# Decode values of a hybrid decoder layer: two samples share one 128-row operand, one value sum per pair, loads issued by ScalarE

## The chip, the cores and the metric

One core of a Trainium2 chip runs the kernel. The metric is device time in microseconds (us) of one execution, lower is better. Engine names: PE (TensorE, matmuls), DVE (VectorE), ACT (ScalarE), POOL (GpSimd), SP (SyncE, which here only issues DMAs).

## What is computed

One inference step of a decoder layer, for a prompt of 256 tokens and for 8 samples with one new token each (264 token columns in all, `T`): a half-step SwiGLU FFN, a combined projection `h @ w_in`, dilated attention in three head groups of four heads, a complex-diagonal SSM, gates, an output projection and a second half-step FFN. The part that is changed is the decode attention of the samples, more exactly its product with the cached values:

```
idx = buf_len + arange(S)[:, None] - arange(n_back + 1)[None, :] * dil
kg, vg = k_all[:, idxc], v_all[:, idxc]
s = einsum('bshe,bsjhe->bhsj', q, kg) * ATT_SCALE
p, lse = masked_softmax_lse(s, valid)
o = einsum('bhsj,bsjhe->bshe', p, vg)
```

For each of the 8 samples and each of the three groups (dilation 1, 4, 16) 128 cached keys and the new one count; the three groups' outputs of a head slot are merged by their softmax denominators. The kernel normalizes over the three groups at once, so the merged output of one sample and one head is a single sum over 3 x 128 cached keys of weight times value (128 wide), plus the new token's term.

## The kernel before

**The slab stream.** All weights pass as slabs of 512 x 256 f32 (512 KB). `put` (L399) on SP issues a slab's load into one of four buffers `raw`; ACT rounds it to `w_hi` (`split_hi`, L611); DVE makes the rest, `w_lo = raw - w_hi` (`split_lo`, L1002); PE does three matmuls for each of 8 tiles (24 in all, `slab_products`, L1440 to L1442). ACT and DVE work on the slab three places ahead of PE (`LEAD`). ACT's split of place j waits until PE is done with the slab before place j, so ACT's body for place j begins about when PE begins slab j.

**The phase `gates_b`.** Four iterations i of eight slabs j (0 to 7). Into them, at fixed places written out by hand in each engine's body, two other pieces of work are threaded, each for k = 2i (half h = 0) and k = 2i + 1 (h = 1).

The SSM piece of block k: PE multiplies the inputs after slab j = 1 or 4 (L1741, `su_done`); ACT copies the product out and prepares states (L843 to L847, `sv_ready`); POOL (L2056 to L2060) and DVE (L1264 to L1267) make the real and the imaginary part of the scan input; DVE runs two scans (L1271, L1273, `scan_ready`), the second after POOL's `zr_ready`; then POOL (L2062, L2064, L2068, `xr_ready`) and DVE (L1282, L1283, L1289, `xi_ready`) turn the scan output into `xs`, with DVE's `w_lo` of a slab (L1002) ahead of its share; PE waits for both and makes the outputs after slab j = 4 or 7 (`y_products`, L1713 and L1719).

The value piece of sample k: SP loads three tiles `vu`, 128 keys x 512 each (L550, 256 KB), at j = 1 and 5; ACT scales the 12 head columns by their weights in `pt_dec` (L828) at j = 0 and 3; POOL adds the three groups in two steps (L2049, L2051) at the head of each half, before its SSM part; PE sums over the 128 keys with four products against a column of ones (L1752) after slab j = 2 and j = 5; DVE adds the new token's term (`add_values`, L1251). There are two sets of three tiles.

The order on each engine is the order of its body: POOL does half 0, then half 1; a wait in it holds all that is behind it. The first phase after `gates_b`, `attn_branch`, waits for `att_lo` (L1299), made on DVE from the samples' attention output.

## Time and profile before

| | |
|---|---|
| median of 3 runs | 2247.19 us (2247.15 to 2248.25) |
| the profiled execution's own time | 2247.63 us |
| its span, first to last instruction | 2244.6 us |
| granted TensorE clock | 1.00 |
| PE / DVE / ACT / POOL busy | 2234.5 / 1373.5 / 995.5 / 488.1 us |
| `gates_b` to the first product of the next phase | 1172.65 to 1294.35 us |

The profile gives, for one execution, the busy time of each engine, the chain of work that ended last, and groups of instructions with their duration and with what ended the idle time before them. Its time lines give start and duration (us) of each instruction. A duration in a time line is from issue to end, so an instruction that stands blocked after its issue shows as a longer one. Matmuls overlap: their spacing counts, not their duration.

### The profile page before, as it was taken

What the parts mean: (1) busy time and instruction counts of PE and PEld (TensorE: products, weight loads), DVE (VectorE), ACT (ScalarE), POOL (GpSimd) and SP (SyncE); (2) the same over time, 40 slices, a digit from 0 to 9 for tenths busy, and PEclk for the clock granted to TensorE, in tenths of its full rate; (3) what the DMA queues carried; (4) which work ended last, traced back from release to release, by engine and by line L of the source; (5) the groups of instructions that cost most, each with busy time, mean ns of one, the idle gap of its engine ahead of it and who ended that gap; (6) DMA issues with size and microseconds to landing.
All of it is one profiled execution on the core that took longest, in us unless ns stands there. A gap on an engine that the chain in (4) does not pass through costs nothing.

```text
span 2244.6 us, 48634 instructions
## 1 busy us (share of the span) xinstructions
PE 2234.5 (100%) x19149; PEld 2223.3 (99%) x19149; DVE 1373.5 (61%) x1434; ACT 995.5 (44%) x1247; POOL 488.1 (22%) x530
## 2 busy tenths in 40 slices
PE   9999999999999999999999999999999999999999
PEld 8999999999999999999999999999999999999999
DVE  7556456665455757876659867665554555545555
ACT  6554334334344544444455665444343343433443
POOL 2587013320000206764306630100000000000000
PEclk9999999999999999999999999999999999999999
DMA  7878678887786688769858875578877788777764
GB/s 226 264 243 259 193 235 271 262 249 239 234 249 202 220 264 262 219 188 298 291 185 285 266 231 182 174 232 251 247 237 226 240 246 256 229 228 242 242 201 147
DMA packets 441036, 528.53 MB, mean 235 GB/s; under 512 B 41360, under 2 KB 421696, under 8 KB 437088
## 3 DMA queue, kind: packets, MB, share of 16 engines
q1 hardware_dynamic: 425600, 508.57, 72.4%
q0 software_dynamic: 3248, 11.62, 1.5%
q10 hardware_dynamic: 12080, 6.83, 1.0%
q8 instruction: 76, 1.25, 0.2%
q14 instruction: 32, 0.26, 0.0%
HBM read 507.80 MB, written 106.09 MB: 273 GB/s over the span
## 4 chain that ended last, share of the span: by engine, by line
PE 97%; DVE 2%; issue 0%; ACT 0%; DMA 0%; ACTq 0%; DVEq 0%
PE pa L1440 31%; PE pa L1441 31%; PE pa L1442 31%; DVE w_lo L1002 1%; PE pb L1618 0%; PE pb L1713 0%; DVE xg_lo L1019 0%; PE pb L1719 0%; PE pb L1678 0%; PE pb L1656 0%; PE pb L1636 0%; PE pb L1752 0%; DMA vec_rows<-in_ffn_norm 0%; DVE x_t L1026 0%; PE pb L1741 0%
## 5 line engine op out<-in xcount | busy, mean ns | idle before, releaser
L1002 DVE TENSOR_TENSOR w_lo<-raw,w_hi 128x1024 fp32r<-128x1024 f32 x735 | 934.7, 1282 | 624.0 <-ACT w_hi L611 620.0
L1440 PE MATMUL pa<-xg_hi,w_hi 128*128 128x264 f32 x3968 | 1135.4, 286 | 1.9 <-DVE w_lo L1002 1.7
L1441 PE MATMUL pa<-xg_lo,w_hi 128*128 128x264 f32 x3968 | 1127.8, 284 | 0.0
L1442 PE MATMUL pa<-xg_hi,w_lo 128*128 128x264 f32 x3968 | 1126.3, 284 | 0.0
L611 ACT ACTIVATE w_hi<-raw 128x1024 fp32r<-128x1024 f32 x735 | 768.8, 1056 | 760.0 <-PE pa L1442 713.9
L1440 PEld LDWEIGHTS pa<-xg_hi,w_hi 128*128 128x128 f32 x3968 | 747.0, 188 | 5.2 <-DVE w_lo L1002 2.5
L1441 PEld LDWEIGHTS pa<-xg_lo,w_hi 128*128 128x128 f32 x3968 | 745.4, 188 | 0.6
L1442 PEld LDWEIGHTS pa<-xg_hi,w_lo 128*128 128x128 f32 x3968 | 745.9, 188 | 0.0
L1441 PE MATMUL pa<-act_lo,w_hi 128*128 128x264 f32 x1632 | 463.9, 284 | 0.0
L1440 PE MATMUL pa<-act_hi,w_hi 128*128 128x264 f32 x1632 | 463.5, 284 | 0.0
L1442 PE MATMUL pa<-act_hi,w_lo 128*128 128x264 f32 x1632 | 463.2, 284 | 0.0
L1440 PEld LDWEIGHTS pa<-act_hi,w_hi 128*128 128x128 f32 x1632 | 307.3, 188 | 0.1
L1442 PEld LDWEIGHTS pa<-act_hi,w_lo 128*128 128x128 f32 x1632 | 306.7, 188 | 0.0
L1441 PEld LDWEIGHTS pa<-act_lo,w_hi 128*128 128x128 f32 x1632 | 306.4, 188 | 0.0
L1848 POOL TENSOR_TENSOR ssq<-ssq,sq_v 128x528 f32<-128x528 f32 x12 | 19.0, 1587 | 367.7 <-ACT sq_v L622 352.3
L735 ACT ACTIVATE act_hi<-hid_v 128x528 f32 (+2 forms) x44 | 28.0, 636 | 158.3 <-DVE hid_v L1165 158.3
L1997 POOL TENSOR_TENSOR silu_v<-up_v,cs 64x264 f32<-64x264 f32 x48 | 66.9, 1394 | 93.0 <-DVE up_v L1198 89.4
L719 ACT ACTIVATE silu_v<-gate_v 128x528 f32<-128x528 f32 (+1 forms) x44 | 28.0, 637 | 108.1 <-DVE gate_v L1157 108.1
L1167 DVE TENSOR_TENSOR act_lo<-hid_v,act_hi 128x528 f32 (+2 forms) x44 | 32.2, 732 | 38.8 <-ACT act_hi L735 38.8
L1058 DVE SCALAR_TENSOR_TENSOR x_t<-pa,x_t 128x528 f32 (+1 forms) x55 | 38.9, 707 | 27.9 <-PE pa L1442 27.8
L2019 POOL TENSOR_TENSOR prod<-ku,qb 128x512 f32<-128x512 f32 x24 | 40.8, 1698 | 46.7 <-DMA qb<-q_dram 31.1
L1047 DVE TENSOR_TENSOR up_v<-pa,rstd 128x528 f32<-128x528 f32 (+1 forms) x44 | 30.5, 693 | 29.7 <-PE pa L1442 29.7
(339 smaller groups left out, 1501.0 us busy)
## 6 DMA issues: line engine op xcount, KB each, us to landing
raw<-in_ffn_w_gate SPq DMA_DIRECT2D x172, 512.0 KB, 4.8
raw<-in_ffn_w_up SPq DMA_DIRECT2D x172, 512.0 KB, 5.0
out_kv_s<-in_cache_kv_w SPq DMA_DIRECT2D x165, 512.0 KB
raw<-in_ffn_w_down SPq DMA_DIRECT2D x160, 512.0 KB, 4.5
raw<-in_w_in SPq DMA_DIRECT2D x152, 512.0 KB, 4.8
raw<-in_w_out SPq DMA_DIRECT2D x32, 512.0 KB, 4.5
tab<-ssm_tab SPq DMA_DIRECT2D x8, 1152.0 KB, 9.1
raw<-in_w_ssm_branch SPq DMA_DIRECT2D x16, 512.0 KB, 4.3
```

What stands on the lines that cost most here:

```text
L611: act.activation(w_hi[:, slot], raw[:, slot], ACT.Copy).then_inc(hi_ready, 1)
L719: act.activation(silu_v[:, 0:w], gate_v[:, 0:w], ACT.Silu).then_inc(silu_ready, 1)
L735: act.activation(act_hi[:, bass.ds(tile0, w), :], hid_v[:, 0:w], ACT.Copy).then_inc(acthi_ready, 1)
L1002: dve.tensor_tensor(w_lo[:, slot], raw[:, slot], w_hi[:, slot].bitcast(f32), ALU.subtract).then_inc(lo_ready, 1)
L1047: return dve.tensor_tensor(out, pa[:, b:b + w, 0:T], rstd[:, None, :].to_broadcast([P, w, T]), ALU.mult)
L1058: dve.scalar_tensor_tensor(x_t[:, bass.ds(2 * c, 2), :], pa[:, b:b + 2, 0:T], scale, x_t[:, bass.ds(2 * c, 2), :], ALU.mult, ALU.add).then ...
L1167: dve.tensor_tensor(act_lo[:, bass.ds(tile0, w), :], hid_v[:, 0:w], act_hi[:, bass.ds(tile0, w), :].bitcast(f32), ALU.subtract).then_inc(a ...
L1440: pe.matmul(out, wh, hi, start=first, stop=False)
L1441: pe.matmul(out, wh, lo, start=False, stop=False)
L1442: return pe.matmul(out, wl, hi, start=False, stop=last)
L1997: pool.tensor_tensor(silu_v[to:to + 64, u], up_v[frm:frm + 64, u], cs[frm:frm + 64, 1], ALU.mult).then_inc(rot_ready, 1)
L2019: pool.tensor_tensor(prod[n % 2][:].rearrange("p h d -> p (h d)"), ku[n % 4][:], qb[n % 3][:], ALU.mult).then_inc(prod_ready, 1)
```

## The change

- A tile `vu[g]` now holds two samples: rows 0 to 63 are sample 2i and rows 64 to 127 sample 2i + 1, and a row holds two keys, p and p + 64, side by side (2 x 512). A tile is filled by two DMAs of 64 rows, 256 KB each.
- The weights `pt_dec` are laid out to match, by four small copies instead of one. ACT still makes 24 scalings an iteration, now 8 at each of j = 0, 2, 3, a group at a time.
- POOL folds the two keys of a row (`vu[g][:, 0] += vu[g][:, 1]`) for each group and adds the groups: five additions an iteration instead of four. One stands ahead of half 0's SSM part, two between the making of the scan input and the use of the scan output of half 0, two ahead of half 1's SSM part.
- PE makes one set of four products for each iteration, after j = 5, against a 128 x 2 matrix `sample_of` that is 1 for the rows of a sample. The set after j = 2 is gone, and `add_values` runs once an iteration, at j = 5.
- In iteration 0 SP loads all three tiles at j = 1 (it loaded three at j = 1 and three at j = 5). In the other iterations SP loads none and no longer waits for `pv_done`: ACT issues the next iteration's loads, two DMAs at each of j = 5, 6, 7, after its split and a wait that the tile is free (`next_values`).
- Four small memsets on DVE at the start fill `sample_of`.

```diff
@@ -260,7 +261,7 @@
     u_t, cs, k_rows, s_rows = tiles(RR, RRN, ("u_t", [P, SC, T]), ("cs", [P, 2, T]), ("k_rows", [P, 2, 512]), ("s_rows", [P, 512]))
     ku = [tile(f"ku{k}", [P, NSLOT * HD], f32, RR + 2048 * k) for k in range(4)]
     RV = RR + RRN - 6 * 2048
-    vu = [tile(f"vu{k}", [P, NSLOT * HD], f32, RV + 2048 * k) for k in range(6)]
+    vu = [tile(f"vu{g}", [P, 2, NSLOT * HD], f32, RV + 4096 * g) for g in range(NG)]
     yt_v, ys_v = tiles(YT, RV - YT, ("yt_v", [P, SC, NT]), ("ys_v", [P, SC, NS]))
     xnew, xtmp, st_rows = tiles(RV, 6 * 2048, ("xnew", [P, 2, 256]), ("xtmp", [P, 3, 256]), ("st_rows", [P, 6, P]))
 
@@ -350,6 +351,11 @@
     att_hi_ready, att_lo_ready, sig_ready, prod_s, m_ready, x_back = sems("att_hi_ready att_lo_ready sig_ready prod_s m_ready x_back")
     yt_ready, yrow_ready, stored = sems("yt_ready yrow_ready stored")
     half_used, last_added, last_moved = sems("half_used last_added last_moved")
+
+    def value_rows(g, b):
+
+        src = caches[g].rearrange("b t (q p r) h d -> b t q p r (h d)", q=2, r=GROUPS[g][1])
+        return src[bass.ds(b, 1), 1, :, :, 0, :].rearrange("o q p c -> (o p) q c")
 
     def q_end(name):
 
@@ -512,6 +518,12 @@
             while tails:
                 shift(*tails.pop(0))
 
+            def load_values(g):
+
+                for half in range(2):
+                    at = slice(64 * half, 64 * half + 64)
+                    sync.dma_start(vu[g][at], value_rows(g, half)).then_inc(vu_loaded[g], 16)
+
             def store_y(k):
 
                 sync.wait_ge(y_read, k + 1)
@@ -531,23 +543,17 @@
             def gates_b(i, ph=PH["gates_b"]):
                 for j in range(8):
                     put(ph, i, j, cols(w_in, 512 * (j % 4), 512, GOFF + D + i * 512 + 256 * (j // 4)))
-                    if j in (1, 5):
-                        h = j // 4
-                        if below(i, 1):
-                            if h == 0:
-                                sync.wait_ge(prod_ready, len(UNITS))
-                                sync.wait_ge(qk_ready, 2 * NH)
-                                sync.wait_ge(rows_stored, ROWS_STORED)
-                                for kv in range(2):
-                                    for g in range(NG):
-                                        dst = new_caches[g][:, kv, GROUPS[g][0] - 1].rearrange("b h d -> b (h d)")
-                                        sync.dma_start(dst, kv_dram[kv, g]).then_inc(stored, 16)
-                                        n_stored[0] += 16
-                        else:
-                            sync.wait_ge(pv_done, 2 * i + h - 1)
-                        for g, (_, dil) in enumerate(GROUPS):
-                            src = caches[g].rearrange("b t (m r) h d -> b t m r (h d)", r=dil)[bass.ds(2 * i + h, 1), 1, :, 0, :]
-                            sync.dma_start(vu[3 * h + g][:], src.rearrange("o m c -> (o m) c")).then_inc(vu_loaded[h], 16)
+                    if below(i, 1) and j == 1:
+                        sync.wait_ge(prod_ready, len(UNITS))
+                        sync.wait_ge(qk_ready, 2 * NH)
+                        sync.wait_ge(rows_stored, ROWS_STORED)
+                        for kv in range(2):
+                            for g in range(NG):
+                                dst = new_caches[g][:, kv, GROUPS[g][0] - 1].rearrange("b h d -> b (h d)")
+                                sync.dma_start(dst, kv_dram[kv, g]).then_inc(stored, 16)
+                                n_stored[0] += 16
+                        for g in range(NG):
+                            load_values(g)
                     if j in (3, 7):
                         h = j // 4
                         if below(i, 1):
@@ -813,20 +819,32 @@
                                pb[:, 2:4, P:P + 144].rearrange("p g (a c) -> p a g c", a=2), ACT.Copy)
                 act.activation(x_fin[:, :, bass.ds(4 * k, 4)], xs[:, :, :, NS + NB], ACT.Copy).then_inc(y_read, 1)
 
+            def next_values(i, g):
+
+                act.wait_ge(*((v_step, 4 * i + 3), (v_sum_ready, i + 1), (pv_done, i + 1))[g])
+                for half in range(2):
+                    at = slice(64 * half, 64 * half + 64)
+                    act.dma_start(vu[g][at], value_rows(g, 2 * i + 2 + half)).then_inc(vu_loaded[g], 16)
+
+            def scale_values(i, g):
+
+                act.wait_ge(vu_loaded[g], 32 * i + 32)
+                if below(i, 1) and g == 0:
+                    act.wait_ge(dec_ready, 1)
+                for q in range(2):
+                    for hh in range(NSLOT):
+                        v = vu[g][:, q, hh * HD:(hh + 1) * HD]
+                        ins = act.activation(v, v, ACT.Copy, scale=pt_dec[:, q, g, bass.ds(NSLOT * i + hh, 1)])
+                ins.then_inc(vs_ready, 1)
+
             def gates_b(i, ph=PH["gates_b"]):
                 for j in range(8):
                     split_hi(ph, i, j + LEAD)
-                    if j in (0, 3):
-                        h = j // 3
-                        k = 2 * i + h
-                        act.wait_ge(vu_loaded[h], 48 * i + 48)
-                        if below(i, 1) and h == 0:
-                            act.wait_ge(dec_ready, 1)
-                        for g in range(NG):
-                            for hh in range(NSLOT):
-                                v = vu[3 * h + g][:, hh * HD:(hh + 1) * HD]
-                                ins = act.activation(v, v, ACT.Copy, scale=pt_dec[:, g, bass.ds(NSLOT * k + hh, 1)])
-                        ins.then_inc(vs_ready, 1)
+                    last = isinstance(i, int) and i == ph.iters - 1
+                    if j in (0, 2, 3):
+                        scale_values(i, max(j - 1, 0))
+                    if j >= 5 and not last:
+                        next_values(i, j - 5)
                     if j == 4 or (j == 7 and not (isinstance(i, int) and i == ph.iters - 1)):
                         read_y(2 * i + j // 5)
                     if j in (1, 4):
@@ -1239,7 +1257,11 @@
                 if (i, j) == (6, 3):
                     dve.wait_ge(dt_done, 1)
                     dve.wait_ge(v_new_ready, 6)
-                    dve.tensor_copy(pt_dec[:].rearrange("p a b -> p (a b)"), pb[:, 3, 0:96])
+                    weights = pb[:, 3, 0:96].rearrange("p (g i s h) -> p g i s h", g=NG, s=2, h=NSLOT)
+                    for sample in range(2):
+                        for q in range(2):
+                            to, frm = slice(64 * sample, 64 * sample + 64), slice(64 * q, 64 * q + 64)
+                            dve.tensor_copy(pt_dec[to, q].rearrange("p g (i h) -> p g i h", h=NSLOT), weights[frm, :, :, sample])
                     dstep(dve.tensor_tensor(att_new[:].rearrange("p g (b h) -> p g b h", b=NS),
                                             pb[:, 3, P:P + 96].rearrange("p (g b h) -> p g b h", g=NG, b=NS), v_new[:], ALU.mult))
                     dstep(dve.tensor_tensor(att_new[:, 0], att_new[:, 0], att_new[:, 1], ALU.add))
@@ -1248,8 +1270,9 @@
             def add_values(k):
 
                 dve.wait_ge(pv_done, k + 1)
-                dve.tensor_tensor(att_v[:, :, bass.ds(NT + k, 1)], pb[:, 0, PV:PV + NSLOT, None],
-                                  att_new[:, 0, bass.ds(NSLOT * k, NSLOT), None], ALU.add).then_inc(pv_read, 1)
+                dve.tensor_tensor(att_v[:, :, bass.ds(NT + 2 * k, 2)], pb[:, 0, PV:PV + 2 * NSLOT].rearrange("p (h s) -> p h s", s=2),
+                                  att_new[:, 0, bass.ds(2 * NSLOT * k, 2 * NSLOT)].rearrange("p (s h) -> p h s", s=2),
+                                  ALU.add).then_inc(pv_read, 1)
 
             def gates_b(i, ph=PH["gates_b"]):
                 for j in range(8):
@@ -1733,23 +1759,19 @@
                         pe.wait_ge(tab_loaded[h], 16 * i + 16)
                         if below(i, 1) and h == 0:
                             pe.wait_ge(u4_loaded, 16 * 48)
-                        else:
-                            pe.wait_ge(pv_read, k)
+                        elif h == 0:
+                            pe.wait_ge(pv_read, i)
                         for m in range(4):
                             for half, g in ((0, 0), (1, 1), (0, 1), (1, 0)):
                                 at, c0 = slice(64 * half, 64 * half + 64), TB_B + m * P + 64 * g
                                 ins = pe.matmul(pb[64 * g:64 * g + 64, half, m * (NS + NB):(m + 1) * (NS + NB)], tab[h][at, c0:c0 + 64],
                                                 u4[at, bass.ds(4 * k + 2 * (m // 2) + g, 1), NS:2 * NS + NB], start=True, stop=True)
                         ins.then_inc(su_done, 1)
-                    if j in (2, 5):
-                        h = j // 4
-                        k = 2 * i + h
-                        pe.wait_ge(v_sum_ready, k + 1)
-                        if below(i, 1) and h == 0:
-                            pe.wait_ge(att_read, NSLOT)
-                        pe.wait_ge(sv_ready, k + 1)
+                    if j == 5:
+                        pe.wait_ge(v_sum_ready, i + 1)
+                        pe.wait_ge(sv_ready, 2 * i + 2)
                         for hh in range(NSLOT):
-                            ins = pe.matmul(pb[:, 0, PV + hh:PV + hh + 1], vu[3 * h][:, hh * HD:(hh + 1) * HD], ones[:, 0:1],
+                            ins = pe.matmul(pb[:, 0, PV + 2 * hh:PV + 2 * hh + 2], vu[2][:, 0, hh * HD:(hh + 1) * HD], sample_of,
                                             start=True, stop=True)
                         ins.then_inc(pv_done, 1)
 
@@ -2042,13 +2064,21 @@
             pool.wait_ge(rows_stored, ROWS_STORED)
             pool.memset(xs[:, :, :, NS:NS + 1], 0.0).then_inc(xs_zero, 1)
 
+            def add(to, other):
+
+                return pool.tensor_tensor(to, to, other, ALU.add)
+
             def gates_b(i):
                 for h in range(2):
                     k = 2 * i + h
-                    pool.wait_ge(vs_ready, k + 1)
-                    pool.tensor_tensor(vu[3 * h][:], vu[3 * h][:], vu[3 * h + 1][:], ALU.add).then_inc(v_step, 1)
-                    pool.wait_ge(v_step, k + 1)
-                    pool.tensor_tensor(vu[3 * h][:], vu[3 * h][:], vu[3 * h + 2][:], ALU.add).then_inc(v_sum_ready, 1)
+                    if h == 0:
+                        pool.wait_ge(vs_ready, 3 * i + 1)
+                        add(vu[0][:, 0], vu[0][:, 1]).then_inc(v_step, 1)
+                    else:
+                        pool.wait_ge(vs_ready, 3 * i + 3)
+                        add(vu[2][:, 0], vu[2][:, 1]).then_inc(v_step, 1)
+                        pool.wait_ge(v_step, 4 * i + 4)
+                        add(vu[2][:, 0], vu[1][:, 0]).then_inc(v_sum_ready, 1)
                     E = tab[h][:, E0:M0].rearrange("p (a c) -> p a c", a=2)
                     pool.wait_ge(sv_ready, k + 1)
                     if not (below(i, 1) and h == 0):
@@ -2058,6 +2088,11 @@
                     pool.tensor_tensor(p_tmp[:, 1], sv[:, 1], E[:, 1], ALU.mult).then_inc(zr_step, 1)
                     pool.wait_ge(zr_step, 4 * k + 2)
                     pool.tensor_tensor(z_in[:, 0], p_tmp[:, 0], p_tmp[:, 1], ALU.add).then_inc(zr_ready, 1)
+                    if h == 0:
+                        pool.wait_ge(vs_ready, 3 * i + 2)
+                        add(vu[1][:, 0], vu[1][:, 1]).then_inc(v_step, 1)
+                        pool.wait_ge(v_step, 4 * i + 2)
+                        add(vu[1][:, 0], vu[0][:, 0]).then_inc(v_step, 1)
                     pool.wait_ge(scan_ready, 2 * k + 2)
                     pool.tensor_tensor(p_tmp[:, 0], z_out[:, 0], E[:, 0], ALU.mult).then_inc(zr_step, 1)
                     pool.wait_ge(zr_step, 4 * k + 3)
```

POOL, the first iteration of `gates_b`, half 0 and the start of half 1 (`vu_114` to `vu_116` are the tiles of the first set, or now of the three groups; `vu_117` to `vu_119` the second set; `tab_96` and `tab_97` the SSM tables of half 0 and half 1). Before:

```order
L2049 TENSOR_TENSOR vu_114<-vu_114,vu_115 128x512
L2051 TENSOR_TENSOR vu_114<-vu_114,vu_116 128x512
L2056 TENSOR_TENSOR p_tmp<-sv,tab_96 128x256
L2058 TENSOR_TENSOR p_tmp<-sv,tab_96 128x256
L2060 TENSOR_TENSOR z_in<-p_tmp 128x256
L2062 TENSOR_TENSOR p_tmp<-z_out,tab_96 128x256
L2064 TENSOR_TENSOR p_tmp<-z_out,tab_96 128x256
L2068 TENSOR_TENSOR xs<-p_tmp 128x4x64
L2049 TENSOR_TENSOR vu_117<-vu_117,vu_118 128x512
L2051 TENSOR_TENSOR vu_117<-vu_117,vu_119 128x512
```

And with the change:

```order
L2069 TENSOR_TENSOR vu_114<-vu_114 128x512
L2086 TENSOR_TENSOR p_tmp<-sv,tab_96 128x256
L2088 TENSOR_TENSOR p_tmp<-sv,tab_96 128x256
L2090 TENSOR_TENSOR z_in<-p_tmp 128x256
L2069 TENSOR_TENSOR vu_115<-vu_115 128x512
L2069 TENSOR_TENSOR vu_115<-vu_115,vu_114 128x512
L2097 TENSOR_TENSOR p_tmp<-z_out,tab_96 128x256
L2099 TENSOR_TENSOR p_tmp<-z_out,tab_96 128x256
L2103 TENSOR_TENSOR xs<-p_tmp 128x4x64
L2069 TENSOR_TENSOR vu_116<-vu_116 128x512
L2069 TENSOR_TENSOR vu_116<-vu_116,vu_115 128x512
```

Between `z_in` and the first `p_tmp` from `z_out` now stand two additions of 128x512 that were not there; the start of the half has one instead of two.

ACT, the first iteration from the split of its first place (j = 0) to that of j = 4. Before:

```order
L611 ACTIVATE w_hi<-raw 128x1024
L828 ACTIVATE vu_114<-vu_114,pt_dec 128x128 x4
L828 ACTIVATE vu_115<-vu_115,pt_dec 128x128 x4
L828 ACTIVATE vu_116<-vu_116,pt_dec 128x128 x4
L851 ACTIVATE att_hi<-att_v 128x256
L611 ACTIVATE w_hi<-raw 128x1024
L843 ACTIVATE sv<-pb 128x256
L844 ACTIVATE s_new<-pb 128x32
L843 ACTIVATE sv<-pb 128x256
L844 ACTIVATE s_new<-pb 128x32
L847 ACTIVATE xs<-x_t 128x4x8 x2
L611 ACTIVATE w_hi<-raw 128x1024 x2
L828 ACTIVATE vu_117<-vu_117,pt_dec 128x128 x4
L828 ACTIVATE vu_118<-vu_118,pt_dec 128x128 x4
L828 ACTIVATE vu_119<-vu_119,pt_dec 128x128 x4
L611 ACTIVATE w_hi<-raw 128x1024
```

And with the change:

```order
L617 ACTIVATE w_hi<-raw 128x1024
L837 ACTIVATE vu_114<-vu_114,pt_dec 128x128 x8
L869 ACTIVATE att_hi<-att_v 128x256
L617 ACTIVATE w_hi<-raw 128x1024
L861 ACTIVATE sv<-pb 128x256
L862 ACTIVATE s_new<-pb 128x32
L861 ACTIVATE sv<-pb 128x256
L862 ACTIVATE s_new<-pb 128x32
L865 ACTIVATE xs<-x_t 128x4x8 x2
L617 ACTIVATE w_hi<-raw 128x1024
L837 ACTIVATE vu_115<-vu_115,pt_dec 128x128 x8
L617 ACTIVATE w_hi<-raw 128x1024
L837 ACTIVATE vu_116<-vu_116,pt_dec 128x128 x8
L617 ACTIVATE w_hi<-raw 128x1024
```

The 8 scalings of the second tile stand behind the split at j = 2, where nothing stood between the splits of j = 2 and 3; 8 stand at j = 3, where 12 stood.

## Rows read from the trace of the kernel before

**Rows 1.** Page, busy time and the chain that ended last

```profile
PE 2234.5 (100%) x19149; PEld 2223.3 (99%) x19149; DVE 1373.5 (61%) x1434; ACT 995.5 (44%) x1247; POOL 488.1 (22%) x530
...
PE 97%; DVE 2%; issue 0%; ACT 0%; DMA 0%; ACTq 0%; DVEq 0%
```

**Rows 2.** Stretches, iteration 1: length, PE PEld DVE ACT POOL, clock, DMA, GB/s

```profile
1203.33:1233.80 30.47, 30.47 (x358) 29.64 (x353) 25.63 (x29) 18.25 (x48) 18.51 (x16) 1.00 0.84 280
```

**Rows 3.** Time line, PE, value products in iteration 1: start, duration, instruction

```profile
1213.03 0.95 PE L1752 MATMUL pb<-ones,vu 128*128 128x1 f32 x8
1213.84 0.37 PE L1440 MATMUL pa<-xg_hi,w_hi 128*128 128x264 f32 x1
1214.04 0.28 PE L1441 MATMUL pa<-xg_lo,w_hi 128*128 128x264 f32 x1
```

**Rows 4.** Time line, PE: SSM inputs and outputs of half 0, iterations 0 to 2

```profile
1178.57 0.73 PE L1741 MATMUL pb<-u,tab 64*64 64x72 f32 x32
...
1189.20 0.64 PE L1713 MATMUL pb<-u,tab 128*128 128x72 f32 x4
...
1209.35 0.73 PE L1741 MATMUL pb<-u,tab 64*64 64x72 f32 x32
...
1219.75 0.56 PE L1713 MATMUL pb<-u,tab 128*128 128x72 f32 x4
...
1239.82 0.73 PE L1741 MATMUL pb<-u,tab 64*64 64x72 f32 x32
...
1250.47 0.64 PE L1713 MATMUL pb<-u,tab 128*128 128x72 f32 x4
```

**Rows 5.** Time line, ACT, iteration 1

```profile
1204.82 3.61 ACT L828 ACTIVATE vu<-vu,pt_dec 128x128 f32<-128x128 f32 x12
...
1210.99 0.43 ACT L847 ACTIVATE xs<-x_t 128x32 f32 x2
1211.29 1.08 ACT L611 ACTIVATE w_hi<-raw 128x1024 fp32r<-128x1024 f32 x1
...
1223.13 0.44 ACT L847 ACTIVATE xs<-x_t 128x32 f32 x2
```

**Rows 6.** Time line, POOL, iteration 1

```profile
1208.51 1.28 POOL L2049 TENSOR_TENSOR vu<-vu,vu 128x512 f32<-128x512 f32 x1 [7.61 <-ACT vu L828]
...
1215.88 1.64 POOL L2062 TENSOR_TENSOR p_tmp<-z_out,tab 128x256 f32<-128x256 f32 x1 [1.21 <-DVE z_out L1273]
1217.60 0.81 POOL L2064 TENSOR_TENSOR p_tmp<-z_out,tab 128x256 f32<-128x256 f32 x1
1218.48 0.81 POOL L2068 TENSOR_TENSOR xs<-p_tmp 128x256 f32<-128x256 f32 x1
1219.25 1.45 POOL L2049 TENSOR_TENSOR vu<-vu,vu 128x512 f32<-128x512 f32 x1
1220.77 2.14 POOL L2051 TENSOR_TENSOR vu<-vu,vu 128x512 f32<-128x512 f32 x1
```

**Rows 7.** Time line, DVE, iteration 1

```profile
1215.14 0.66 DVE L1273 TENSOR_TENSOR_SCAN z_out<-tab,z_in 128x256 f32<-128x256 f32 x1
1215.72 1.19 DVE L1002 TENSOR_TENSOR w_lo<-raw,w_hi 128x1024 fp32r<-128x1024 f32 x1
...
1218.72 0.85 DVE L1289 TENSOR_TENSOR xs<-d_tmp 128x256 f32<-128x256 f32 x1
...
1219.56 2.21 DVE L1002 TENSOR_TENSOR w_lo<-raw,w_hi 128x1024 fp32r<-128x1024 f32 x1
```

**Rows 8.** DMAs into `vu` from issue to landing, and the issue time on SP

```profile
L550 SPq DMA_DIRECT2D vu<-in_cache_kv_w x24: 333/432/887, 1160.2 to 1265.2; - x24
...
DMA to landing us min/median/max: 2.7/4.6/8.2
```

**Rows 9.** Time line, ACT's queue: a DMA issue at the start of the kernel

```profile
0.76 0.45 ACTq L885 DMA_DIRECT2D x_rows<-in_x_sample  x1
```

**Rows 10.** Time line, PE, first product of `attn_branch`

```profile
1294.35 0.39 PE L1440 MATMUL pa<-att_hi,w_hi 128*128 128x264 f32 x1 [0.97 <-DVE att_lo L1299]
```

20 lines of the change are left out of this document (12 added, 8 removed).

## The prediction

> **What bounds the kernel now.** I read first the page: PE is busy for all of the span and holds 97% of the chain that ended last [rows 1]. So what PE is spared is gained, and what PE waits is lost, unless something else ends the wait. Then the stretches of the phase that is changed: in iteration 1, PE is busy for the 30.47 us, DVE for 25.63 (five sixths) and the DMA engines for 0.84 of the time, ACT and POOL for some 18 [rows 2]. DVE is the engine with little to spare. Last the time lines, for one question: where do PE's threaded pieces wait for others, and by how much are the others early?
>
> The answer is in the SSM outputs of half 0 (`y_products`, after slab 4). From PE's SSM inputs (after slab 1) to these outputs PE has three slabs and one set of value products to do. In iteration 1 this takes 10.40 us; in iterations 0 and 2 it takes 10.63 and 10.65 [rows 4]; iteration 3 has 10.40 again. The 0.23 and 0.25 us more are waits. POOL ends its share of `xs` at 1218.48 + 0.81 = 1219.29 and DVE its share at 1218.72 + 0.85 = 1219.57 [rows 6, 7], and PE begins the outputs at 1219.75 [rows 4]. So this handover has no slack: DVE is 0.2 us early, POOL 0.5. All that the change puts on POOL or DVE ahead of `xs` in half 0 comes out on PE.
>
> **The change part by part.**
>
> *PE's value products.* One set begins at 1213.03; the next slab product follows at 1213.84 and its successor at 1214.04 [rows 3]. Without the set that successor would stand one spacing (0.12) after 1213.03, so a set costs 1.01 - 0.12 = 0.89 us. Two columns instead of one change nothing I can see in such a duration: between a product of 264 columns and one of 1 column the spacing hardly differs. Four sets go (the ones after slab 2): 3.6 us less on PE. But they go from inside the very interval that ends with the wait for `xs`: PE comes 0.89 us earlier to a handover that had 0.2. What is left of the 3.6 is decided by `xs`.
>
> *POOL's additions in half 0.* I count from `sv_ready` (t = 0), which in iteration 1 is 1210.99 + 0.43 = 1211.42, 2.07 us after PE's SSM inputs began [rows 4, 5]; the change leaves that, since ACT waits there for PE, and its 8 scalings at j = 0 end sooner than 12.
>  - ACT's split at j = 2 begins at 1211.29 and holds ACT for about 1.05 us; 8 scalings at 3.61/12 = 0.30 us take 2.41 [rows 5]. The second tile is scaled at 1214.75, t = 3.35.
>  - POOL has made its part of the scan input by about t = 2.7 (three rounds of 0.88, below) and must now stand in wait for that tile, then do two additions of 128x512, and only then the three operations that make `xs`.
>  - An addition takes 1.28 us where DVE was idle, 1.45 and 2.14 where DVE was at work [rows 6]. The pair at 1219.25 shows why: POOL's addition runs to 1220.70, DVE's `w_lo`, issued at 1219.56, ends at 1221.77, 1.07 later; POOL's next, issued at 1220.77, ends at 1222.91, 1.14 after that [rows 6, 7]. They go one after the other, not side by side. Likewise POOL's L2062 takes 1.64 instead of 0.81 behind a `w_lo` of 1.19 [rows 6, 7].
>  - So I lay the work in a line. DVE's second scan ends at 1215.80, t = 4.4, after a POOL part that began late behind two additions [rows 7]; with one addition there I put it at 4.0. Addition 1 to 5.1; `w_lo` (1.07), which DVE has ahead of its share of `xs`, to 6.2; addition 2 (1.14) to 7.3. Then three rounds in which DVE and POOL take turns: L2064 ends at 1218.41 and L2068 at 1219.29, 0.88 a round [rows 6], so 2.65 in all and POOL's `xs` at 9.95. From the end of an `xs` to PE's start it took 1219.75 - 1219.57 = 0.18 with DVE last; with such a handover, and a little off for the rounding, PE begins at t = 10.2.
>  - That is 2.07 + 10.2 = 12.27 us after the SSM inputs, against 10.63, 10.40, 10.65, 10.40 now: +1.64, +1.87, +1.62, +1.87, together **+7.0 us**. The 3.6 us of the value products are in this already: PE waits some 2.7 us in each iteration, 0.89 of which it would have worked.
>
> The bounds of this term. Below, POOL never waits for DVE: 3.35 + 0.1 for the handover, two times 1.35, three times 0.88, 0.15 to PE, 8.9: 10.9 us after the inputs, +0.3, +0.5, +0.3, +0.5 = +1.5 us. Above, each addition and L2062 take their longest (1.45, 2.14, 1.64): 10.9, which is 12.9 after the inputs, +9.6 us. I take the laid-out line, since the rows of iteration 1 show the taking of turns to a hundredth. The Trainium skill's page "SBUF — State Buffer", section "Who interferes with whom", says the same: a DVE instruction with two SBUF inputs and a GpSimd instruction that reads SBUF exclude each other for the whole instruction. By that rule the sum is +7.0, by operations that share freely +1.5.
>
> *Half 1.* POOL's two additions stand ahead of its SSM part as before and end about t = 14.5; the next `sv_ready` comes 3.8 us after the outputs began (1223.13 + 0.44 against 1219.75 [rows 4, 5]), at 14.0. POOL and DVE start about 0.5 late against it, and DVE was 0.2 ahead of PE at the outputs after slab 7: between 0 and 0.3 us an iteration, and I put it at 0. The value products after slab 5 need the sum some 5 us after the outputs began and find it.
>
> *The end of the phase.* The first product of `attn_branch` waited 0.97 us for DVE's `att_lo` [rows 10]. DVE gets to it behind the same SSM part; of a longer wait on PE before it, up to 0.5 us may come back here. Taken as 0, against the one above.
>
> *DMA.* The same bytes move. Iteration 0's second three tiles come earlier on SP, before slab 2; SP then stood waiting for the attention output, so they fall into a gap. Later, ACT issues six DMAs an iteration. An issue takes 0.45 us on ACT's queue, 0.43 on SP's [rows 8, 9], and ACT idles 12 of the 30.5 us [rows 2], against 2.7 for six issues: hidden. The first tile's pair goes out at ACT's place 5 and is scaled at place 0: three slabs of 24 spacings (0.12) and the outputs of half 1 (1.9) later, 10.6 us. The 8 scalings would end at 1207.2 and the split behind them at 1208.3, while PE's inputs end only at 1210.1 [rows 4, 5]: 1.9 us more before `sv_ready` suffers, 12.5 in all. One DMA landed in 4.6 us in the middle, 8.2 at most [rows 8]. Two in a row are 9.2: hidden, with 3.3 to spare; two of 8.2 are not. The skill's page "DMA: Bandwidth & Descriptors", section "Rules for kernel authors", speaks against this part: two transfers to the two partition halves serialize and one of 128 partitions is to be preferred. By it the 9.2 holds, and no time is lost on PE.
>
> *The rest.* DVE's four copies for `pt_dec` instead of one, 0.2 us each, stand some places before their use; the memsets at the start lie under the load that the first transpose waits for; `add_values` drops four operations of 0.15 us from DVE, behind `xs`. Nothing.
>
> Sum: the profiled execution would go from 2247.63 to 2254.6 us. It lies 0.44 above the median of the runs; against the median of 2247.19 I give **2254.2 us**. A difference under 0.2% (4.5 us) can't be told from none.
>
> **The rivals.**
>  - *The value products' saving shows (faster).* POOL's additions would have to be done by the time PE arrives, 10.40 - 0.89 = 9.51 us after the inputs, t = 7.4. From there on the saving decides: 3.6 us, with the 0.5 us of waits in rows 4 and the 0.97 at the end if they go too: -5.1, 2242.1 us. For it speaks that PE is 97% of the chain. Against it, the lower bound of POOL's line is t = 8.9. It needs ACT's second tile much earlier than its place after the split allows. Chance 0.06.
>  - *DVE and POOL do not hold each other up.* +1.5: 2248.7 us. For it: in the rounds of 0.88 us POOL's operations keep 0.81, near what they take at any time. Against it: rows 6 and 7. Chance 0.19, with values between this and my line up to 2251.7.
>  - *The value loads come late.* Half-height tiles from a second queue, against 0.84 busy DMA engines, land as the slowest now, 14 us for a pair: 1.5 us beyond the 12.5, in three iterations, +4.5 on top: 2258.7 us. For it: the landing times spread over 2.7 to 8.2. Against it: the median. It would show as ACT waiting for `vu`. Chance 0.10.
>  - My forecast, 2254.2 us: 0.65.
>
> **How the numbers follow.** The range holds the forecast with its bounds (2248.7 to 2256.8) and reaches to the late loads: 2248.4 to 2258.7; outside lie the faster case and the tails. Slower by over 0.2% (above 2251.7) are the forecast and the late loads, 0.75; within 0.2% the free sharing, 0.19; faster 0.06.
>
> **What would show it.** In the profile after: PE idle before L1713 of half 0, 2 to 3 us in each iteration, released by POOL's `xs`; from SSM inputs to outputs 12.3 us; the two middle additions ending near t = 5.1 and 7.3, the second with over 2 us; four value sets of 0.89 us; no wait of ACT for `vu`; half 1 without a wait over 0.3. If that interval is under 11 us, the taking of turns was wrong; if PE does not wait there at all, the whole argument is. If the loss stands at another line, it is a rival's.

## The result and the profile after

| | before | after |
| --- | --- | --- |
| median, us | 2247.17 (2246.81 to 2248.25, 4 runs) | 2261.35 (2260.46 to 2263.29, 4 runs) |
| ratio, 95% interval | | 1.0062 (1.0050 to 1.0074) |
| profiled execution, us | 2247.63 | 2261.29 |
| span, us | 2244.6 | 2259.5 |

The change costs 14.2 us. The sign is the forecast's; the size is twice it (+7.0) and lies outside the range, whose upper end was 11.5 above the median of before.

The page of after, busy time and the chain that ended last, beside [rows 1]:

```profile
PE 2237.3 (99%) x19117; PEld 2225.0 (98%) x19117; DVE 1377.3 (61%) x1437; ACT 995.4 (44%) x1247; POOL 490.9 (22%) x534
...
PE 92%; DVE 2%; issue 2%; POOL 1%; DMA 1%; ACT 1%; ACTq 0%; POOLq 0%; SPq 0%; DVEq 0%
```

PE has 32 instructions fewer and is no longer the whole chain. The waits of PE in the changed phase: who waited for whom, us in all, times, longest:

```profile
PE pb L1739 <- POOL xs L2103: 8.3, 3, 3.8
PE pb L1739 <- DVE xs L1312: 2.4, 1, 2.4
PE pa L1466 <- DVE att_lo L1322: 0.8, 1, 0.8
```

So PE waits at the forecast's place, the outputs of half 0, once in each iteration. POOL's `xs` ends three of the waits, as forecast, and DVE's the one of iteration 0. The time line of PE in iterations 0 and 1 (L1767 inputs, L1739 outputs, L1774 value products), beside [rows 3, 4]:

```profile
1180.16 0.73 PE L1767 MATMUL pb<-u,tab 64*64 64x72 f32 x32
1192.26 0.76 PE L1739 MATMUL pb<-u,tab 128*128 128x72 f32 x4 [2.43 <-DVE xs L1312]
1200.74 0.95 PE L1774 MATMUL pb<-small,vu 128*128 128x2 f32 x8
...
1215.38 0.73 PE L1767 MATMUL pb<-u,tab 64*64 64x72 f32 x32
1227.38 0.67 PE L1739 MATMUL pb<-u,tab 128*128 128x72 f32 x4 [2.33 <-POOL xs L2103]
...
1232.91 0.95 PE L1774 MATMUL pb<-small,vu 128*128 128x2 f32 x8
```

The four intervals from inputs to outputs are 12.10, 12.00, 13.47 and 11.85 us: +1.47, +1.60, +2.82 and +1.45 on before, +7.3 together. That leaves some 6 us of the phase's loss unexplained. They come after the wait. Stretches of after (length, busy time of PE, PEld, DVE, ACT, POOL, granted clock, DMA, GB/s):

```profile
1192.00:1200.00 8.00, 7.74 (x90) 7.22 (x91) 6.83 (x8) 2.58 (x9) 5.54 (x5) 0.57 0.54 167
...
1226.00:1234.00 8.00, 6.62 (x106) 6.32 (x107) 7.23 (x8) 3.49 (x10) 7.69 (x7) 1.00 0.56 176
...
1260.00:1268.00 8.00, 6.98 (x84) 6.46 (x85) 6.43 (x7) 2.58 (x9) 5.17 (x5) 0.57 0.69 193
...
1193.00:1199.00 6.00, 6.00 (x81) 5.58 (x81) 4.87 (x6) 2.58 (x9) 3.62 (x4) 0.50 0.45 133
```

And the whole phase of before:

```profile
1172.65:1294.35 121.70, 120.57 (x1370) 116.94 (x1369) 104.00 (x114) 74.39 (x193) 73.97 (x64) 1.00 0.85 275
```

After the waits of iterations 0 and 2 the granted clock of TensorE is 0.57 over eight microseconds. Inside them (last row of after) it is 0.50, the lower of its two levels (1.2 GHz in place of 2.4), for 6.8 us each time, from 1192.6 and from 1260.9 (summed over windows of 1 us). After those of iterations 1 and 3 it stays at 1.00, and so it does in all of this phase of before. What it costs can be read: from the outputs to the value products PE takes 1200.74 - 1192.26 = 8.48 us in iteration 0 and the same in iteration 2, against 5.53 in iterations 1 and 3 (1232.91 - 1227.38). That is 2.95 twice, 5.9 us. 7.3 + 5.9 = 13.2, and from the first SSM inputs to the first product of `attn_branch` (1309.20 in after, [rows 4, 10] for before) it is 13.3 us longer. The other 1.6 us of the span lie before it (a first load that landed 1.0 us later, the rest in a phase with the same instructions), and I take them for the spread of single executions; no run tests that.

The third interval has a cause of its own. The time line of ACT, iteration 2:

```profile
1248.84 1.06 ACT L617 ACTIVATE w_hi<-raw 128x1024 fp32r<-128x1024 f32 x1 [2.79 <-DMA raw<-in_w_in]
1249.80 0.37 ACT L861 ACTIVATE sv<-pb 128x256 f32<-128x256 f32 x1
```

A weight slab was late; its split stands ahead of the `sv` copies on ACT, which were therefore later, and the interval is 1.47 us longer than in iteration 1. The DMAs into `vu`, beside [rows 8]:

```profile
L827 ACTq DMA_DIRECT2D vu<-in_cache_kv_w x18: 602/607/704, 1196.6 to 1274.4; - x18
...
DMA to landing us min/median/max: 3.9/8.3/11.7
```

They take 0.61 us to issue and 8.3 to land, where 0.45 and 4.6 had been read [rows 8, 9].

### The profile page after: what moved, and what is told of

Read it like the earlier page. It is cut to its first block, busy times and chain, and to the rows that moved or that the text cites. A ratio compares the mean times of both kernels' runs of the same rounds, so it can differ in the third digit from the quotient of the medians.

```text
span 2259.5 us, 48583 instructions
## 1 busy us (share of the span) xinstructions
PE 2237.3 (99%) x19117; PEld 2225.0 (98%) x19117; DVE 1377.3 (61%) x1437; ACT 995.4 (44%) x1247; POOL 490.9 (22%) x534
## 3 DMA queue, kind: packets, MB, share of 16 engines
q8 instruction: 76, 1.25, 0.2%
## 4 chain that ended last, share of the span: by engine, by line
PE 92%; DVE 2%; issue 2%; POOL 1%; DMA 1%; ACT 1%; ACTq 0%; POOLq 0%; SPq 0%; DVEq 0%
PE pa L1466 30%; PE pa L1467 29%; PE pa L1468 29%; DVE w_lo L1020 1%; DMA raw<-in_ffn_w_down 1%; PE pb L1644 0%; POOL vu L2069 0%; DMA raw<-in_w_in 0%; PE pb L1739 0%; POOL p_tmp L2097 0%; DVE xg_lo L1037 0%; ACT w_hi L617 0%; DMA vec_rows<-in_ffn_norm 0%; PE pb L1704 0%; PE pb L1745 0%
```

## The experiments

An "interval" is always the one from SSM inputs to outputs in half 0, iterations 0 to 3; before has 10.63, 10.40, 10.65, 10.40. Each median (us) stands beside that of before on the same chip. A "fall" is a stretch at a granted clock of 0.50. Experiments 2, 4 and 6 and the first and third run of 5 leave part of the value sum out.

**1. POOL's two additions, put into before.**

```diff
                     if h == 0:
+                        for n in range(2):
+                            pool.wait_ge(*((spare_step, 2 * i + 1) if n else (zr_ready, k + 1)))
+                            pool.tensor_tensor(p_tmp[:], p_tmp[:], sv[:], ALU.add).then_inc(spare_step, 1)
+                        pool.wait_ge(spare_step, 2 * i + 2)
```

> Kernel before, with one thing added: two POOL additions of 128x512 (on scratch, results not used for the output of the additions' own operands) between the scan input and the use of the scan output of half 0, where the change has its two middle additions. What it computes in the SSM part of half 0 is not changed, since the scratch is overwritten. Theory A (the two additions on POOL delay xs and PE waits for it): from SSM inputs to outputs of half 0 some 11.4 to 11.9 us instead of 10.4 to 10.6, so +4 to +6 us, 2251 to 2253 us; the wait of PE stays under 1.5 us and the granted clock at 1.00. Rival B (the loads cost it): no change, 2247 us.

Measured: 2261.95 against 2247.87, ratio 1.0064 (1.0047 to 1.0081). Intervals 12.63, 12.38, 12.72, 12.47, +8.1 in all. The place was forecast rightly, the size was not (+4 to +6 and a clock of 1.00). Nothing but the additions is changed, and they alone cost 14 us, falls of the clock included. That this equals the whole change is in part chance, for here three of the four waits are followed by a fall, in the change two:

```profile
PE pb L1714 <- POOL xs L2074: 5.9, 3, 2.2
PE pb L1714 <- DVE xs L1290: 2.1, 1, 2.1
```

```profile
1192.00:1200.00 8.00, 7.93 (x92) 7.46 (x93) 6.95 (x7) 2.58 (x9) 5.66 (x5) 0.57 0.82 273
1228.00:1236.00 8.00, 8.00 (x120) 7.69 (x119) 7.93 (x9) 3.65 (x10) 5.39 (x6) 1.00 0.81 265
1260.00:1266.00 6.00, 5.53 (x84) 5.06 (x85) 4.91 (x6) 1.79 (x9) 3.70 (x4) 0.72 0.97 295
1294.00:1302.00 8.00, 7.42 (x88) 6.95 (x89) 7.02 (x8) 2.59 (x9) 5.69 (x6) 0.57 0.54 166
```

**2. The change without them.**

```diff
-                    if h == 0:
-                        pool.wait_ge(vs_ready, 3 * i + 2)
-                        add(vu[1][:, 0], vu[1][:, 1]).then_inc(v_step, 1)
-                        pool.wait_ge(v_step, 4 * i + 2)
-                        add(vu[1][:, 0], vu[0][:, 0]).then_inc(v_step, 1)
```

> Changed kernel without the two middle additions on POOL (the second keys of group 1 and the values of group 0 are left out of the samples' sums); layout, loads and all else as in the change. Theory A: PE does not wait for xs in half 0, the interval is 9.5 us, no clock drop, and the saving of four sets of value products shows: 2243 to 2244 us. Rival B (half-height loads from a second queue hold up the slabs): it stays near the changed kernel, 2255 us or more.

Measured: 2251.65 against 2247.87, ratio 1.0020 (1.0010 to 1.0030). Intervals 9.79, 10.95, 12.14, 11.01. 9.79 is the forecast's 10.40 - 0.89 with a quarter more: in iteration 0 the saving on the value products is there. In the others something is late, and it isn't POOL's additions. Waits of ACT from 1200 to 1290 us:

```profile
ACT w_hi L617 <- DMA raw<-in_w_in: 10.1, 4, 3.8
```

Weight slabs are late, by up to 3.8 us. Neither forecast is met. The intervals are 1.8 us above before in all, and the wait of iteration 2 (2.48 us) is followed by a fall of 3.4 us that costs 1.5. So the change has a second cost: the time is about 4 us above before in place of 3.6 us below it. In the full change, with its longer iterations, slabs are late by 1.6, 2.8 and 1.5 us too, and only the one of iteration 2 lengthens an interval.

**3. The loads back on SP's queue**, at SP's places 4, 5 and 6, additions in place.

> Changed kernel with the value loads of iterations 1 to 3 issued by SP again, between its slabs (j = 4, 5, 6), the same two DMAs of 64 rows. If sharing the DMA engines between two queues makes the slabs late (ACT waited 6 us in all for slabs in iterations 1 to 3), these waits go, iteration 2 has its interval at 12.0 instead of 13.5 us, and its clock drop goes with it: 2257 us. If not, no change: 2261 us. Rival B in full: 2250 us or less.

Measured: 2259.33 against 2247.87, ratio 1.0053 (1.0036 to 1.0070). The slab waits of iterations 1 to 3 are gone and the intervals are even, 11.83, 11.99, 11.99, 11.86 (+5.6), with two falls of the clock, in iterations 1 and 2. So iteration 2's interval came out as forecast, 12.0, but its fall did not go. The time lies between the two forecasts (2257 and 2261), and against the change (ratio 1.0062) the difference is not resolved.

**4. Experiments 2 and 3 together.**

> The change with its value loads back on SP's queue and without the two middle additions of POOL (the second keys of group 1 and all of group 0 are left out of the value sum). Theory (the two additions delay the SSM input, and the wait they make costs a second time through the granted clock; the queue of the loads adds the rest): all four intervals from SSM inputs to outputs in half 0 are 9.5 to 9.9 us, PE waits under 0.5 us there, no stretch of half 0 after an output at a granted clock under 0.9, and 2242.5 to 2245 us, some 3 us less than before, which is what the shorter value products save. Rival (the queue plays no part): the same intervals as the run without the two additions and loads on ACT's queue, 9.8 to 12.1, and 2251 us.

Measured: 2252.97 against 2248.17, ratio 1.0023 (1.0013 to 1.0032). Intervals 9.83, 10.29, 11.65, 12.62. The theory fell; the rival's time is near, but not its way, for the lateness has moved: ACT no longer waits for slabs but for values.

```profile
ACT vu L836 <- DMA vu<-in_cache_kv_w: 10.4, 5, 4.3
```

**5. Is it the shape of the loads?** Three runs. First, the same as experiment 4 with each load cut by keys, one DMA into all 128 rows (`vu[g][:, q]` from two samples) in place of 64 rows of both keys.

> The run without the two middle additions and with loads on SP's queue, its value loads cut the other way: one DMA for each of the two keys into all 128 rows, instead of one for each of the two samples into 64 rows (same bytes, same tiles; the second keys of group 1 and all of group 0 are left out of the value sum, as there). Theory (a load into 64 rows costs more than one into 128, 0.6 us to issue and 6 to 8 us to land against 0.33 and 4, and that made the waits of 2.0 to 4.3 us for values): issue 0.35 us, landing 4 to 5 us, ScalarE no longer waits over 1 us for values, intervals 9.8 to 10.3 us in all four iterations, 2243 to 2245 us. Rival (values are late because three tiles in place of six come free late): the same waits, 2252 us.

Measured: 2346.48 against 2247.72, ratio 1.0441: 99 us slower, which no theory had. SP's queue, and a stretch in which those loads run (below it, before's):

```profile
1160.92 20.04 SPq L524 DMA_DIRECT2D vu<-in_cache_kv_w  x6
```

```profile
1165.00:1175.00 10.00, 10.00 (x86) 10.00 (x85) 1.30 (x2) 1.06 (x1) 0.12 (x1) 1.00 0.13 50
```

```profile
1165.00:1175.00 10.00, 10.00 (x86) 10.00 (x86) 4.16 (x4) 4.59 (x8) 0.12 (x1) 1.00 0.67 232
```

A share of 0.13 of 16 DMA engines is two of them. The outermost extent of these DMAs is 2 (the samples), and the 256 KB seem to be dealt out by it; no run varies that extent alone. PE then waits up to 23 us for a table that stands behind these loads in the queue, so this run says nothing on the question asked. The change's own layout and the sum in a later iteration, both with this cut, gave 2349.28 and 2355.17 us (1.0449 and 1.0479); for the first this had been expected:

> The change with its loads on SP's queue and cut by keys, one DMA into all 128 rows each, whole computation. Theory (what is left over before is POOL's two additions and what follows from the wait): issue 0.35 us, intervals 11.8 to 12.0 us as with loads by samples, PE waits of 2.2 us, one or two stretches at half clock, 2256 to 2260 us. Rival (the shape of the loads drives the loss): under 2252 us.

Second, before with each load as two DMAs of 64 rows of one key:

> The kernel before with each of its value loads issued as two DMAs of 64 rows, on SP's queue. Theory (a load into 64 rows costs issue time and DMA time even where nothing else is changed): landing of the last of a set 1 to 4 us later than in before, the DMA engines busier in the half-0 stretches, but the six tiles give room: PE waits stay under 0.5 us and the time is 2247 to 2249 us. Rival (such loads delay the slabs themselves): ScalarE waits over 1 us for slabs in two iterations or more, 2251 us or more.

Measured: 2247.76 against 2247.72, ratio 0.9999 (0.9990 to 1.0009), intervals 10.64, 10.40, 10.66, 10.40, as before. Loads into 64 rows cost before nothing that can be measured. Third, experiment 4 with such loads:

> The run without the two middle additions and with loads on SP's queue, each load cut into two DMAs of 64 rows of one key, the form that cost before nothing (the second keys of group 1 and all of group 0 are left out of the value sum). Theory (a DMA of 64 rows of two keys takes the DMA engines longer for the same bytes, and that made the value waits of 2.0, 3.0 and 4.3 us): the values are waited for under 1 us, intervals 9.8 to 10.3 us in all iterations, clock 1.00 throughout, 2243 to 2246 us. Rival (three tiles in place of six come free too late): the same waits and about 2252.5 us.

Measured: 2253.97 against 2247.07, ratio 1.0031 (1.0019 to 1.0042). Intervals 10.77, 10.53, 10.89, 14.75; ACT waits 13.2 us for values, 6.4 at the longest. So neither shape removes the lateness, and where the buffers give room 64 rows cost nothing. The full change with these loads gave 2262.05 (1.0069), intervals 12.86, 12.01, 11.99, 12.88, no better than experiment 3; the sum in the next iteration with them 2265.90 (1.0081).

**6. Is it the start of the loads?** Before has six tiles and issues three loads at 1187.26 that are scaled at 1204.82, 17.6 us later, and the next three at 1203.15 for 1214.19, 11.0 us. With three tiles, experiment 4 issues the first pair at 1199.91, and ACT, ready at about 1205.2, has it at 1207.18. So experiment 4 again, each load one or two slabs earlier:

```diff
-                    if j in (4, 5, 6) and not below(i, 1):
-                        g = j - 4
+                    for g in ((0, 1), (2,))[j - 3] if j in (3, 4) and not below(i, 1) else ():
```

> The run without the two middle additions and with loads on SP's queue (loads by samples, the second keys of group 1 and all of group 0 left out of the value sum), with the loads issued at SP's slab positions 3, 3 and 4 in place of 4, 5 and 6, that is at 1195 to 1200 us in place of 1200 to 1206. Theory (the loads start too late before their use, and so make ScalarE wait 2.0 to 4.3 us): no wait for values over 1 us, intervals 9.8 to 10.3 us in all iterations, clock 1.00 throughout, 2243 to 2246 us. Rival (the DMA engines are full there, and whatever is moved earlier makes a slab late): ScalarE waits for slabs instead, 2250 us or more.

Measured: 2251.36 against 2246.78, ratio 1.0018 (1.0008 to 1.0027). Each theory had half of it right. Intervals 10.01, 10.66, 9.90 and then 13.95. No wait for values is left, and iteration 2, at 9.90, is 0.75 us under before. But slabs are late instead. Waits of ACT, 1200 to 1290 us, and its time line in iteration 3:

```profile
ACT w_hi L622 <- DMA raw<-in_w_in: 12.6, 6, 5.8
```

```profile
1274.07 1.06 ACT L622 ACTIVATE w_hi<-raw 128x1024 fp32r<-128x1024 f32 x1 [5.82 <-DMA raw<-in_w_in]
```

One slab 5.82 us late gives PE a wait of 4.28 us, and the clock falls after it (0.50 from 1284 to 1290 us).

**7. The clock.** Ten transposes of PE, on data that nobody reads, ahead of the outputs of half 0; then twenty, with the loads on SP:

```diff
+                    if j == 4:
+                        pe.wait_ge(sv_ready, 2 * i + 1)
+                        for _ in range(20):
+                            pe.transpose(pb[:, 2, 304:432], ident[:], ident[:])
```

> Changed kernel with ten 128x128 transposes on PE, into unused PSUM columns, ahead of the SSM outputs of half 0: some 2.5 us of work an iteration where PE stood idle 2.4. Theory C (the two stretches at a granted clock of 0.50 follow PE's standing idle): clock 1.00 throughout the phase, the wait before the outputs nearly gone but the interval still 12.0 us, and 5 to 6 us less than the changed kernel: 2255 to 2256 us, faster by more work. Rival D (the clock falls for another cause): 2261 us or a little more, with the 0.50 rows still there.

Measured: 2260.81 against 2247.87, ratio 1.0062 (1.0045 to 1.0079). Inconclusive: ten took only 1.25 us, waits of 1.13, 2.70, 1.24 and 1.44 us remained, and the clock fell after the second and the third.

> The change with loads on SP's queue, and twenty idle transposes of about 0.125 us each on PE ahead of the outputs of half 0, inside the wait of 2.2 to 2.3 us for the SSM input. Theory (it is PE's idleness ahead of the outputs after which the granted clock falls to half): intervals stay at 11.8 to 12.1 us, PE no longer waits more than 0.5 us, the granted clock stays at 1.00 after the outputs, and the two losses of 2.95 us go: about 2253.5 us. Rival (the fall of the clock has another cause): stretches at 0.50 remain after one or two of the outputs, about 2259 us.

Measured: 2257.31 against 2248.17, ratio 1.0040 (1.0027 to 1.0054). PE and the outputs in iteration 2, and the stretches around the outputs of all four iterations:

```profile
1252.92 2.35 PE L1754 MATMUL pb<-ident 128*128 128x128 f32 x20
1255.42 0.67 PE L1736 MATMUL pb<-u,tab 128*128 128x72 f32 x4 [0.15 <-POOL xs L2104]
```

```profile
1188.00:1200.00 12.00, 11.99 (x153) 11.45 (x152) 11.33 (x12) 4.26 (x11) 10.40 (x10) 1.00 0.62 211
1220.00:1232.00 12.00, 11.84 (x152) 11.29 (x151) 11.19 (x12) 4.46 (x11) 10.40 (x10) 1.00 0.81 270
1252.00:1264.00 12.00, 11.85 (x151) 11.30 (x151) 11.18 (x12) 4.79 (x12) 10.40 (x10) 1.00 0.90 229
1286.00:1298.00 12.00, 9.29 (x106) 8.53 (x105) 10.53 (x10) 5.60 (x18) 9.07 (x9) 0.72 0.73 234
```

In iterations 0 to 2 the outputs come as late as in experiment 3 (intervals 11.87, 12.02, 12.01), PE works where it had waited, and the clock stays at 1.00. In iteration 3 the values were 4.1 us late, PE waited 2.71 us in spite of the transposes, and the clock fell. In this profile both falls of experiment 3 are gone and one new one is there, with a wait for values that experiment 3 did not have. The median is 2 us under experiment 3's and not 6, and even the 2 are not resolved. That filling PE's wait keeps the clock up is suggested by iterations 0 to 2 and not shown: unfilled waits of 2.16 to 2.34 us were followed by a fall in five of ten cases over all runs, so three without a fall would come by chance one time in eight.

**8. Can the saving be had?** The sum is added one iteration later: POOL folds and adds group 2 at the head of the next iteration, PE's products follow the next SSM inputs, and the loads are on SP's queue.

> The change's layout of the values with the whole sum computed, but the group sums of a pair of samples are added in the iteration that follows (POOL's additions at its head, ahead of nothing that the SSM input waits for; PE's value products behind the SSM inputs; loads on SP's queue). Theory (only the place of POOL's two additions cost time, the layout saves 0.9 us a set on PE): intervals in half 0 of 9.6 to 10.4 us plus the products that now stand in them, no PE wait over 0.7 us, no stretch at half clock, 2243 to 2245 us, 3 us less than before. Rival (the additions cost wherever they stand, because POOL has no room in an iteration): a wait of 1.5 us or more shows at the SSM input or at the gates' input in at least two iterations, and 2252 us or more.

Measured: 2264.76 against 2248.17, ratio 1.0078 (1.0064 to 1.0092). Intervals 9.80, 13.51, 13.83 and 13.11. ACT waited up to 5.5 us for values, in every iteration after the first, so the theory was not put to its test. With group 0's loads two places earlier:

> The sum added in the next iteration, whole computation, with group 0's loads issued at SP's position 3 in place of 5, some 5 us earlier. If the late load of group 0 alone held it up: ScalarE's wait of 5.1 us at the head of an iteration goes, PE waits in half 0 under 1.5 us, under 2256 us. If the other groups' loads hold it up as well: over 2258 us.

Measured: 2257.24 against 2246.78, ratio 1.0045 (1.0028 to 1.0061). Iterations 0 to 2 have intervals of 10.01, 10.41 and 10.40, no wait of PE over 0.6 us and a clock of 1.00. So with the additions out of the handover POOL's work costs no wait there, as the theory of the run before had it. The last iteration (12.77) loses all: ACT waits up to 6.6 us for values, and PE has a wait of 2.22 us, two falls of the clock, and 2.13 us for the last sum, which has no later iteration to go to:

```profile
1282.63 0.93 PE L1743 MATMUL pb<-u,tab 128*128 128x72 f32 x4 [2.22 <-DVE xs L1318]
1296.33 1.77 PE L1778 MATMUL pb<-small,vu 128*128 128x2 f32 x8 [2.13 <-POOL vu L2073]
1304.84 0.39 PE L1470 MATMUL pa<-att_hi,w_hi 128*128 128x264 f32 x1 [1.33 <-DVE att_lo L1326]
```

The time lies between the two forecasts. No version that I ran beats before.

## Why the prediction was right and where it was wrong

**POOL's additions, the term of +7.0: right in mechanism, some 1.1 us too large, and near the measured +7.3 by luck.** The line laid out gave 12.27 us for every iteration. Measured are 12.10, 12.00 and 11.85, and 13.47 where the late slab adds 1.4. Without that slab the additions cost +5.9, and +5.6 in experiment 3, where no slab is late; the rest of the +7.3 belongs to the DMA term below. Time lines of POOL and DVE in iteration 1 of after, where `sv_ready` is about 1217.45:

```profile
1220.81 1.70 POOL L2069 TENSOR_TENSOR vu<-vu 128x512 f32<-128x512 f32 x1 [0.53 <-ACT vu L837]
1222.58 2.15 POOL L2069 TENSOR_TENSOR vu<-vu,vu 128x512 f32<-128x512 f32 x1
...
1226.54 0.78 POOL L2103 TENSOR_TENSOR xs<-p_tmp 128x256 f32<-128x256 f32 x1
```

```profile
1221.33 2.25 DVE L1020 TENSOR_TENSOR w_lo<-raw,w_hi 128x1024 fp32r<-128x1024 f32 x1
```

The additions end at t = 5.1 and 7.3, to the tenth as laid out, `xs` at 9.9 (laid out 9.95), and PE begins at 9.9 (10.2), so most of the excess is the 0.25 us allowed for the handover. `w_lo`, issued at 1221.33, takes 2.25 us where it took 1.19 in this place before [rows 7], and ends 1.07 after the first addition, as laid out: the two engines take turns. Experiment 1, with the additions alone, gives +8.1, since there PE also keeps its value products. The lower bound of +1.5, for engines that share freely, does not fit any of these runs.

**The price of PE's wait: the step that failed.** The prediction priced a wait of PE at its own length ("PE waits some 2.7 us in each iteration, 0.89 of which it would have worked"). It left out what the wait does to the rate of the work behind it: two waits of the four were followed by 6.8 us at half the clock, which cost 2.95 us more each, +5.9 us, most of the 7.2 us missed. How many of the four it would be could not have been told, and still can't: experiment 1 had three. Before could not have shown the price, as its clock never fell in the phase, but no bound was set in its place: POOL's additions got an upper and a lower one, this term neither. The remainder is 0.3 us in the intervals (1.4 for the slab less 1.1 for the additions) and about 1 us that I can't place in the phase.

**The value products: right in size, and of no use.** Eight products of two columns take 0.95 us, as those of one column [rows 3], and four sets are gone. Experiments 2, 4 and 6 show the interval 0.6 to 0.8 us shorter than before where the inputs are nearly in time (9.79, 9.83, 10.01, 9.90). PE still stands in them for a moment; in experiment 2, iteration 0:

```profile
1189.70 0.28 PE L1468 MATMUL pa<-xg_hi,w_lo 128*128 128x264 f32 x1
1190.11 0.64 PE L1739 MATMUL pb<-u,tab 128*128 128x72 f32 x4
```

The spacing of 0.41 us in place of 0.12 is 0.29 of waiting, and 9.79 less that is 9.5, the forecast's 10.40 - 0.89.

**The DMA term of 0: wrong, with a small price here.** It put an issue at 0.45 us and two landings at 9.2; they were 0.61 and, for one alone, 8.3. The 12.5 us of room did hold the values, for ACT never waited for `vu` in after. What the prediction did not ask is whose landing the loads would delay: the slabs on the other queue. That wait of 2.79 us made iteration 2's interval 1.4 longer than its neighbours', +1.4 us for a term put at 0. The rival of late loads named the place wrongly in after, but rightly in experiments 4 and 5. Its price did not follow from its own rows either: one after the other, two landings of 8.2 are 16.4 us and not 14, which would have put it at some 2266 us.

**The faster rival, 2242.1 us, was too generous.** It asked only that POOL's additions be done in time. Experiments 2, 4, 6 and the last part of 5 take them away, and the time is 2251.4 to 2254.0 us, never below before. On ACT's queue or early on SP's the slabs are late, late on SP's the values are. My reading is that with half the tiles a load can't start until the one before it is used, and that the DMA engines have no gap there for it. That is argued and not shown: no run has this layout with more tiles, and all these runs also issue all of an iteration's loads within 7 to 12 us, where before issues them in two groups of three, some 15 us apart.

**Half 1 and the end: right.** Half 1's intervals are 10.34 us where the clock is 1.00, as before, and the wait for `att_lo` is 0.80 against 0.97.

What stays open is the cause of the falls, and why a wait of some 2 us is followed by a fall in one iteration and not in the next; the section below has the numbers.

## What to carry to other kernels

Price a new wait of the engine that bounds the kernel at more than its length: look whether the clock behind it stays up, and put the cost of a fall into the range. When a change halves the buffers of a stream, compare the time from issue to use with the landing times, and ask what else the moved transfers will run beside. An engine's free time says little on what work added to it costs: POOL is idle for four fifths of the kernel and two fifths of this phase, and yet of the 3.2 us that the two additions took in experiment 1 some 2.0 came out on PE in each iteration, because they stand inside a handover without slack.

## What the runs showed of the hardware that I had not expected

- The granted clock of TensorE fell to 0.50 after many of PE's waits in this phase, and in no run without a wait of PE before it. At the outputs of half 0 it stayed up after waits of 1.44 us, 1.66, 1.82, 2.16, 2.19 (twice), 2.32 and 2.33 us, and after those under 1.2 us, of 1.23, 1.28 and 1.34 us too; it fell after waits of 1.24 us (behind ten transposes), 1.91, 1.98, 2.07, 2.16, 2.22, 2.32 (twice), 2.34 and all the longer ones, from 2.43 us up. Equal waits went either way.
- A fall had one of two lengths. In all runs but the three with loads cut by keys, where PE stands for up to 23 us, the 27 falls around this phase lasted 3.4 us (ten of them) or 6.8 us (seventeen), summed over windows of 1 us. Where it can be read at the outputs of half 0, a short one cost 1.5 us and a long one 2.6 to 3.0.
- In 10 us in which SP issued nothing but DMAs of 256 KB with an outermost extent of 2, about two of the 16 DMA engines were busy (0.13 and 50 GB/s), and 24 such DMAs cost the kernel 99 us.
- On SP's queue a DMA of 64 rows of two keys took 0.61 us to issue in the median (experiment 3), one of 128 rows of one key 0.43 (before), for the same 256 KB; one of 64 rows of one key, half the bytes, took 0.55 (second run of experiment 5).
